# Mixer of a hybrid decoder layer: one mixer stream with TensorE transposes, against separate QKV, attention and dense streams with DMA transposes

## The reference

```python
x = x + 0.5 * swiglu(rmsnorm(x, ffn1_norm), ...)        # 1024 -> 2816 -> 1024
h = rmsnorm(x, mix_norm)
q_lat, kv_lat, k_rope, xc, gB, gC, gates = split(h @ w_in)
q = rmsnorm(q_lat) @ w_uq                               # 8 heads of 96
k, v = rmsnorm(kv_lat) @ w_uk, rmsnorm(kv_lat) @ w_uv   # 8 heads of 64
q, k = head-wise rmsnorm, rotary on the last 32 of 96 (k_rope is shared by the heads)
y_a = causal softmax(q k^T / sqrt(96)) v @ w_proj_attn
y_b = (gB * conv3(gC * xc)) @ w_proj_conv
x = x + (sigmoid(gA) * y_a + sigmoid(gB') * y_b) @ w_out
x = x + 0.5 * swiglu(rmsnorm(x, ffn2_norm), ...)
```

## Time and profile before

| what | value |
| --- | --- |
| median of 3 runs | 3841.93 us (3838.07 to 4163.69) |
| profiled execution | 3882.15 us, span of its slowest core 3880.6 us |
| spans of the 8 cores | 3815.0 to 3880.6 us |
| busy share of the span: TensorE, VectorE, ScalarE, GpSimd | 87%, 37%, 25%, 6% |
| chain that ended last | TensorE 74%, VectorE 12%, DMA 5% |
| moved over the span | 335.58 MB by DMA, mean 86 GB/s |

### The profile page before, as it was taken

One profiled execution on the slowest core, in us unless ns is written; L12 is line 12 of the kernel. 1 busy time (PEld: TensorE's weight loads), 2 busy tenths in 40 slices (PEclk: granted clock), 3 DMA queues, 4 the chain that ended last, 5 costly groups with the idle time before them and its releaser, 6 DMA issues.

```text
span 3880.6 us, 41321 instructions; the slowest of 8 cores (3815.0 to 3880.6 us)
## 1 busy us (share of the span) xinstructions
PE 3379.5 (87%) x15840; PEld 1551.1 (40%) x15840; DVE 1436.7 (37%) x2293; ACT 973.2 (25%) x1477; POOL 244.2 (6%) x350
## 2 busy tenths in 40 slices
PE   6799999999977778787787878778788999999999
PEld 3343444444433334333343333334333444444444
DVE  2121121122155574645446565654532222212211
ACT  2121111111122242331622223252442112211110
POOL 2000000000010100001001010101110000000000
PEclk9898898899986889898898989899989999999999
DMA  9823441531122314132141423314457111111110
GB/s 185 147 63 60 91 74 41 94 76 60 55 91 74 120 66 155 53 115 85 44 141 63 149 70 116 111 55 144 109 115 178 66 66 44 49 39 65 55 44 33
DMA packets 84861, 335.58 MB, mean 86 GB/s; under 512 B 9792, under 2 KB 9920, under 8 KB 81856
## 3 DMA queue, kind: packets, MB, share of 16 engines
q1 hardware_dynamic: 72000, 279.80, 21.5%
q0 software_dynamic: 12672, 53.16, 9.7%
HBM read 335.74 MB, written 68.81 MB: 104 GB/s over the span
## 4 chain that ended last, share of the span: by engine, by line
PE 74%; DVE 12%; DMA 5%; POOL 3%; ACT 3%; issue 2%; another core or an unknown queue 0%; SPq 0%; ACTq 0%; POOLq 0%; DVEq 0%
PE banks L626 71%; DVE rec L1022 5%; POOL hr L919 3%; DMA axr_99<-x 2%; DMA axr_100<-x 1%; DVE qf L937 1%; PE banks L736 1%; PE banks L945 1%; DMA xin_69<-x1s 1%; PE banks L947 1%; ACT SQ L903 1%; DMA xin_70<-x 1%; DVE kf L934 1%; DVE attnT_124 L1023 1%; ACT SQ L905 0%
## 5 line engine op out<-in xcount | busy, mean ns | idle before, releaser
L626 PE MATMUL banks<-awd,aact 128*128 128x512 bf16 x1408 | 328.5, 395 | 11.7 <-DMA awd<-ws 11.7
L626 PE MATMUL banks<-cwd,cact 128*128 128x512 bf16 x1408 | 309.1, 379 | 0.0
L1022 DVE RECIPROCAL rec<-banks 64x512 f32<-64x512 f32 x64 | 214.8, 3356 | 53.3 <-PE banks L626 52.7
L626 PEld LDWEIGHTS banks<-awd,aact 128*128 128x128 bf16 x1408 | 140.8, 101 | 185.2 <-issue 66.8
L626 PE MATMUL banks<-QT,KT 128*128 128x512 bf16 (+3 forms) x640 | 194.9, 392 | 12.4 <-ACT pt_113 L998 8.7
L626 PEld LDWEIGHTS banks<-cwd,cact 128*128 128x128 bf16 x1408 | 136.7, 98 | 160.5
L945 PE MATMUL banks<-identb,qf 128*128 128x128 bf16 x256 | 30.8, 295 | 170.5 <-DVE qf L937 170.5
L729 POOL TENSOR_SCALAR ssq<-ssq 128x1 f32<-128x1 f32 x96 | 18.5, 192 | 2553.4 <-ACT xn_71 L727 2182.8
L998 ACT ACTIVATE pt_113<-banks,negM 128x1024 bf16<-128x1024 f32 (+2 forms) x110 | 110.9, 1008 | 223.0 <-PE banks L626 222.8
L772 ACT ACTIVATE asg_96<-banks 128x512 f32<-128x512 f32 x88 | 52.5, 597 | 455.7 <-PE banks L626 455.7
L772 ACT ACTIVATE csg_153<-banks 128x512 f32<-128x512 f32 x88 | 52.5, 597 | 439.4 <-PE banks L626 439.4
(11 more groups left out here) (400 smaller groups left out, 5604.1 us busy)
## 6 DMA issues: line engine op xcount, KB each, us to landing
ring_126<-wms SPq DMA_DIRECT2D x16, 896.0 KB, 4.4
ring_127<-wms SPq DMA_DIRECT2D x16, 896.0 KB, 4.4
ring_128<-wms SPq DMA_DIRECT2D x16, 896.0 KB, 4.4
ring_129<-wms SPq DMA_DIRECT2D x16, 896.0 KB, 4.6
ring_126<-wms SPq DMA_DIRECT2D x16, 768.0 KB, 4.4
ring_127<-wms SPq DMA_DIRECT2D x16, 768.0 KB, 4.5
ring_128<-wms SPq DMA_DIRECT2D x16, 768.0 KB, 4.3
ring_129<-wms SPq DMA_DIRECT2D x16, 768.0 KB, 4.5
```

Source lines behind the costliest of these rows:

```text
L626: fns.append(lambda e, o_=o_, l_=l_, r_=r_, st=st, sp_=sp_: e.matmul(o_, lhsT=l_, rhs=r_, start=st, stop=sp_))
L1022: yield op("dve", lambda e: e.reciprocal(out=rec.t[po:po + 64, :], in_=bk(OB)[pr:pr + 64, :]), [d_bank[OB]], rec.d, c_psum(512))
```

## The change

`norm_stream` now scales and multiplies the gain in one VectorE operation, and a DMA transpose from SBUF to SBUF, issued by SP, writes `hT`. All other transposes go the same way: the latents (`qk5` to `lt5`), `qf` to `QT`, `kf` to `KT`. TensorE has no transposes left. `attn` becomes a stream of its own (`a_stream`, PSUM banks 0 to 2), `qkv` keeps `m_stream` (banks 3 and 4), with two `QT` buffers so that the QKV work of the next group can run under the attention of this one. The front of tile t+1 is put before the middle of tile t. Attention goes by single key tiles of 512 columns. At the end of a head ScalarE copies the sums and VectorE the numerators out of the accumulator; for two heads together VectorE takes one reciprocal of 128x512 in four pieces, and GpSimd multiplies. GpSimd takes over the mask, the `qf` product, half of `kf` and the small operations of the norms. The ring has 10 buffers of 1024 columns in place of 4 of 4096. The FFN 2 weights are cast to `wms` during the mixer, one piece in every three steps of `d_stream`, and loaded by SP as bfloat16 after it. FFN residual loads are issued during the gate and up matmuls, not after them. `schedule` looks at up to 24 operations of every stream, and takes the first free one per engine if it touches nothing that an earlier one does; the cost constants are new.

```diff
@@ norm_stream
-            yield op("act", lambda e, i=i: e.activation(out=xn[i].t[:], in_=xin[i].t[:], func=AF.Copy, scale=rr.t[:, i, 0:1]),
-            fns = [lambda e, k=k, i=i: e.transpose(out=tv[:, k, :], in_=xn[i].t[:, k * 128:(k + 1) * 128], identity=identb.t[:])
...
+            yield op("dve", lambda e, i=i: e.scalar_tensor_tensor(out=xn[i].t[:], in0=xin[i].t[:], scalar=rr.t[:, i, 0:1], in1=grow.t[:],
+                                                                  op0=ALU.mult, op1=ALU.mult),
+            yield dma("sp", s_tx[i], lambda e, i=i, h=h, tt=tt: e.dma_start_transpose(out=h.t[:, :, tt * 128:(tt + 1) * 128], in_=xn[i].t[:]),
...
@@ streams
+    def a_stream():
+        yield Wait(lambda: "f1.done" in flags)
+        for g in range(NG):
+            yield Wait(lambda g=g: f"m.q.{g}" in flags)
+            for o_ in attn(g):
+                yield o_
...
@@ qkv: front, back and their order
+        BA, BB, BQ, BK, BV = 3, 4, 3, 3, 4
...
+            yield dma("sp", s_t5[b], lambda e: e.dma_start_transpose(out=lt5[b].t[:], in_=qk5[b].t[:]), qk5[b].d, lt5[b].d, 128 * 1280)
...
+            yield op("pool", lambda e: e.tensor_tensor(out=qf.t[:], in0=T1, in1=hq.t[:, b, 0:8, None].broadcast_to([128, NH, 128]),
+            yield dma("sp", s_tq, lambda e: e.dma_start_transpose(out=QT[hb].t[:, :, tsl], in_=qf.t[:].rearrange("p h d -> p (h d)")),
...
+            yield dma("sp", s_tk, lambda e: e.dma_start_transpose(out=KT.t[:, st], in_=kf.t[:].rearrange("p h d -> p (h d)")),
...
         for tt in range(TPG):
+            if tt + 1 < TPG:
+                for o_ in front(tt + 1):
+                    yield o_
+            if tt == 0 and gi == 0 and g > 0:
+                yield Wait(lambda: f"m.a.{g - 1}" in flags)
             for o_ in mid(tt):
                 yield o_
@@ attn: the end of a head
-                yield op("dve", lambda e: e.reciprocal(out=rec.t[po:po + 64, :], in_=bk(OB)[pr:pr + 64, :]), [d_bank[OB]], rec.d, c_psum(512))
...
+                yield op("act", lambda e: e.activation(out=R.t[po:po + 64, :], in_=bk(OB)[pr:pr + 64, :], func=AF.Copy),
+                yield op("dve", lambda e: e.tensor_copy(out=X.t[po:po + 64, :], in_=bk(OB)[po:po + 64, :]), [d_bank[OB]], X.d, c_dve(512))
+                if hh % 2:
+                    for q in range(4):
+                        yield op("dve", lambda e, qs=qs: e.reciprocal(out=R.t[:, qs], in_=R.t[:, qs]), R.d, R.d, 80 + 6.4 * 128)
...
@@ cast_w, FFN 2 pieces
+        for n, F in ffn_plan("f2"):
+            at = 3 * i
+            yield Wait(lambda at=at: f"d.c.{at // 16}.{at % 16}" in flags)
...
+            yield dma("pool", s_wm[n], lambda e, off=off, mo=mo, F=F: e.dma_start(out=wm_d[:, mo:mo + F], in_=ws_d[:, off:off + F]),
```

More of the change, by code:

```diff
@@ L326, in schedule, with fill, settle, heads @@
     def schedule(self, streams):
-        live = [[i, g, None] for i, g in enumerate(streams)]
+        WIN = 24
+        live = [[i, g, [], False] for i, g in enumerate(streams)]
+        def fill(s):
+            while len(s[2]) < WIN and not s[3]:
+                try:
+                    s[2].append(next(s[1]))
+                except StopIteration:
+                    s[3] = True
+        def settle(s):
+            moved = False
+            while True:
+                fill(s)
+                if not s[2]:
+                    break
+                it = s[2][0]
+                if isinstance(it, Do):
+                    it.fn()
+                elif isinstance(it, Wait) and it.cond():
+                    pass
+                else:
+                    break
+                s[2].pop(0)
+                moved = True
+            return moved
+        def heads(s):
+            seen = set()
+            rd, wr = set(), set()
+            for k, it in enumerate(s[2]):
+                if isinstance(it, Do):
+                    continue
+                if isinstance(it, Wait):
+                    if it.cond():
+                        continue
+                    break
+                r_ = {id(d) for d in it.reads}
+                w_ = {id(d) for d in it.writes}
+                if it.eng not in seen:
+                    seen.add(it.eng)
+                    if not (w_ & rd) and not (w_ & wr) and not (r_ & wr) and not self.blocked(it):
+                        yield k, it
+                rd |= r_
+                wr |= w_
+                if len(seen) == 5:
+                    break
         while live:
@@ L967, in attn @@
         sc = 1.0 / math.sqrt(DQK)
-        steps = [(hh, kp) for hh in range(NH) for kp in range(nkt // 2)]
+        steps = [(hh, kt) for hh in range(NH) for kt in range(nkt)]
         n = len(steps)
-        OB = 4
+        OB = 2
+        Q = QT[g % 2]
+        dQ = d_QT[g % 2]
         def geo(kt):
@@ L1093, in conv @@
                 b0 = nb()
-                for o_ in dense(b0, [(wv[:, 0, k, :], h[:, k, :]) for k in range(8)], [r.d, d_hT[hb]]):
+                yield rwait()
+                r = take(f"conv{c}")
+                for o_ in dense(b0, [(r.t[:, 128 * k:128 * k + 128], h[:, k, :]) for k in range(8)], [r.d, d_hT[hb]]):
                     yield o_
+                yield freed()
                 for o_ in pend:
@@ L1138, in proj @@
                 b0 = nb()
[L1139 removed]
+                yield rwait()
+                r = take(f"m4{c}")
+                for o_ in dense(b0, [(r.t[:, 128 * k:128 * k + 128], h[:, k, :]) for k in range(8)], [r.d, d_hT[hb]]):
                     yield o_
+                yield freed()
                 for o_ in pend:
```

795 lines of the change are left out of this document (413 added, 382 removed).

## The result

The changed kernel takes 3416.84 us (median of four runs, 3411.03 to 3419.49), against 3841.93 us for the kernel before in the same session (median of three, 3838.07 to 3857.93). The ratio, of the means, is 0.8882, with a 95% interval of 0.8848 to 0.8916: faster by 11%. The forecast was 3280, the range 3130 to 3610. Runs in which one die of the chip ran at a lower clock are left out of every time and ratio here; for one experiment, which is named, that leaves two runs and no interval.

What follows compares the result with a forecast made beforehand. TensorE was taken as the only engine near a bound, with most idle time in the mixer. Start 40, FFN 1 984, mixer 1367 and FFN 2 921 sum to 3312 us profiled, 3277 for runs, stated as 3280; range 3130 to 3610.

Steps and rivals of the forecast that it cites:

- the mixer at 1367 us: Mixer: 1292 us of matmuls at 0.935 of full pace plus 75 us idle, against 1876 before.
- the bin called forecast: Whole kernel: the summed estimate holds and the runs take 3130 to 3410 us, chance 0.66.
- waits or clock: Whole kernel: waits return where DMAs land late, or the clock stays low; 3410 to 3610 us, chance 0.15.
- signs: Mostly mixer: idle near 75 us, clock 0.9 or above, transposes landing in 2 to 6 us, DMA share about 0.7.
- The start, 40 us with ends of 34 and 50: Time until the first FFN 1 matmul, with DMA transposes replacing the last tile's TensorE transposes; 32.3 us before.
- The words on SP: Mixer: a transpose waiting for its input holds ring loads behind it on SP; ten buffers, 17 us, cover that.
- up to 28 us of a burst are covered: FFN 1: residual loads issued 8 and 4 steps early cover this much of a cast burst, leaving 10 us idle.
- FFN 1's matmuls, 974 us: FFN 1: matmul time without transposes, keeping the measured 0.935 of full pace.
- the rival of a clock of 0.81 through the mixer: Mixer: matmuls take 1491 us plus 75 idle, 3475 us for the runs; within the 0.15 for waits or clock.
- What was to be late next: Mixer: score to exponential to `Vc` handoff with masks, 35 us, and pipeline filling, some 40 us; together 75 us idle.
- the rival that ends slower: Mixer: a DMA transpose takes above 10.7 us a tile; at 11.9 the runs take 3985 us; chance 0.09.
- The factor 0.9896: Whole kernel: median of runs over profiled execution before, 3841.93 / 3882.15, used to turn 3312 us into 3277.

Runs made afterwards that it cites:

- e1_hold: Changed kernel with the fourth and later FFN 1 weight loads waiting for the last transpose of group 0: 3376.86 us, ratio 0.8802 to the kernel before.
- e9_pace: Changed kernel with each weight cast at the start waiting until the cast two before it has landed: 3372.82 us, ratio 0.8795 to the kernel before.
- best1: Changed kernel with mixer casts spread, weight casts paced, roots of groups 0 and 1 off GpSimd, group 2's norm behind the last weight: 3263.48 us, ratio 0.8532.
- e2_te0: Changed kernel with the four tiles of group 0 of FFN 1 transposed on TensorE, all others by DMA: 3388.08 us, ratio 0.8843 to the kernel before.
- e4_xr3: Changed kernel with three residual buffers instead of two, casts still in bursts: 3382.87 us, ratio 0.8822 to the kernel before.
- e3b_spread: Changed kernel with each of the twenty mixer casts in FFN 1 waiting for the Silu of its step: two runs, 3329.75 and 3322.89 us.
- the repeat: Changed kernel run again, its order and waits unchanged because an edit to spread casts had no effect: 3420.18 us, ratio 0.8917 to the kernel before.
- e7_plain: Changed kernel with the mixer's DMA transposes for latents, QT and KT replaced by plain DMA copies: 3396.49 us, ratio 0.8875 to the kernel before.
- e6_te_mix: Changed kernel with the mixer's transposes for latents, QT and KT back on TensorE: 3439.55 us, ratio 0.8968 to the kernel before.

## Why the prediction was right, and where it was off

The direction and the range held, and so did its main term: the mixer at 1367 us, measured 1356. The result lies 7 us outside the bin called forecast (up to 3410, chance 0.66), in that of waits or clock (0.15). Two steps failed, and that two paces were taken too low, by 53 and 46 us, hid part of it. This was luck: without them the same sum would be 3520 us on the profile, 3483 for the runs.

Of its signs, five held: the DMA share in the mixer (0.71), the clock there (0.97), the landing of a transpose, no wait on `qf`, and GpSimd not busy all through. One sign of being wrong did come: TensorE waits for `hT`, 130.5 us, though not in the mixer. FFN 1 was not free of waits for residual tiles either.

- **The start, 40 us with ends of 34 and 50: 130.5.** It had seen that all DMA engines are taken (share 0.96), and took from the earlier trace rows a landing of 8.1 us. The x loads of that very place would have told it no more: before the first matmul they landed in 5.5 to 10.7 us. The step that failed is that a DMA transpose may stand there at no price but a landing. Its issue held SP for up to 29.7 us, and loads behind one took 33 to 37. The words on SP, that a transpose holds the ring loads behind it, were applied to the mixer, where it did little harm (7.7 us of waits for a ring buffer), and not to the start. e1_hold, e9_pace and best1 show the one half of the cause, the same transposes with fewer casts in the way, e2_te0 and the kernel before the other, the same casts without transposes.
- **FFN 1's idle time, 10 us: 93.** The step that failed is "up to 28 us of a burst are covered". Loads issued earlier are of use for tiles 0 and 1 only; tiles 2 and 3 wait for a store from the same buffer, the store for SP, which a transpose held, and all of them for the burst. The diff showed it: three buffers became two. e4_xr3 gives the buffer a quarter of the waits; e3b_spread shows that without the burst none of them come.
- **FFN 1's matmuls, 974 us: 921.** The pace of before (0.935) was kept as the safe choice; the granted clock was 0.95 here, and 1.00 through FFN 1 without its gaps (e3b_spread). The pace of before was that of a slow core: in the same execution six of the eight cores ran this stretch (35 to 1070 us) at a clock of 0.96 or 0.97, and cores 4 and 5 at 0.92; the row is core 5's. Why these two were slower stays open.
- **The mixer.** Of the 520 us 101 are the transposes, 306 idle time, and 112 a faster pace, at a clock of 0.97 where it was 0.88. Pace 0.935 was too careful again (1292, measured 1246), idle 75 too low (110, or 104 by the repeat), and the rival of a clock of 0.81 through the mixer did not come. What was to be late next was named in part: exponentials and masks came to 26 us, but the two largest waits, on `kf` and `convT` (13.0 and 12.7), were not named. GpSimd's part held as well: the `qf` product took 1.91 us for the 2.6 estimated, and GpSimd is busy for 604 us of the 1418.
- **The crossbar.** 2 us a tile was taken, between 0.8 and 11.9; 1.9 came out, and 3.1 to 5.2 us to landing for the 2 to 6 said, so the rival that ends slower had no ground. The Trainium skill, "VectorE: DVE Perf Modes", The three transpose paths, has 1309 ns for a block, an estimate of 10.5 us for eight in a row: this case does not bear that out. The Trainium skill, "Advanced Engine Details and Errata", X-Bar Transpose (TRN2), has them as fast as plain DMAs: the time of e7_plain agrees, the DMA share does not (1.9 us of all engines for a tile, 0.4 for a copy).
- **Which part does it.** The working gave the transposes 100.9 us and the end of the `qf` waits to the DMA path. e6_te_mix corrects this: 20 to 33 us hang on the crossbar, and the wait on `qf` goes with the streams, whoever transposes. The forecast of the mixer was right in size, but gave the transposes' new way some 240 of its 520 us too much.
- **From the profile to the runs.** The factor 0.9896 came from one execution of before that was 1% above its median. The profiled execution after (3418.33) is at its median, so 35 of the 140 us between 3277 and the result are this factor, read on the same slow core as the pace of FFN 1; the other 105 are the sum itself (+90, +83, -53, -46, +35, -5).

## What to carry to other kernels

Before work moves to a DMA queue, look at what else fills the DMA engines at each place where it is issued, above all at the start and where casts go out together. The row of another kind of transfer will not do, even from the same place: plain loads took 5.5 to 10.7 us at this start, and the transposes put there held their queue for up to 29.7. Where no row shows the new kind beside the casts, give that place wide bounds. Spread large casts by a wait on real progress; a schedule that spaces them only in its own estimate lets them go out in bursts on an engine that has nothing else to wait for. When a wait is put on an in-order queue, list what stands behind it first: three of these runs (e1_hold, e2_te0, e9_pace) moved a stall to another engine's queue.

## What was not expected of the hardware

- The issue of a DMA transpose takes SP 1.23 us where most plain loads and stores took 0.3 to 0.6; with casts filling the DMA engines it held SP for 22.86, 26.90 and 29.69 us. Loads of 512 KB behind one took 33.3 to 37.0 us; under the same weight casts without transposes, in the kernel before, they took 5.5 to 11.9, but for one behind two other loads.
- In the first 130 us a packet of the casting queue took 0.83 x 16 x 130 / 4896 = 0.35 us of an engine, one of SP's 0.065 us, and the shares stood at 83.0% to 18.3%. In the kernel before SP's queue had 18.8% and moved 7.38 MB with it in 2253 packets, in place of 5.42 MB in 5855. That the many small packets of the transposes are why they and the loads take so long fits these numbers; no run tests it.
- A gap shows in the clock behind it. After the 31.2 us of idle time the next 16 matmuls took 5.40 us instead of 3.45, at a granted clock of 0.66 in the mean (its levels are 1.2 and 2.4 GHz), and then 1.00 again. The windows behind that gap in the changed kernel:

```profile
277.90:283.30 5.40, 5.39 (x16) 1.89 (x16) 1.02 (x2) 0.60 (x1) 0.00 (x0) 0.66 0.65 192
283.50:289.00 5.50, 5.39 (x25) 2.52 (x27) 1.79 (x3) 0.60 (x1) 0.00 (x0) 1.00 0.59 190
```
